# Split operands for the channel sums, a stacked gate product, and first terms on ScalarE in a two-block fp32 model

## The reference, cut to what matters

```python
def rwkv7_mixer(z, mu, w0, w2, a0, a2, g2, k_k, k_a, r_k, lnx_w, lnx_b):
    z = z + (z_prev - z) * mu                 # z_prev: z one token earlier
    r, k, v, w_low, a_low, g_low = split(z)   # 1024, 1024, 1024, 64, 64, 160
    ...
    g = jax.nn.sigmoid(g_low) @ g2            # 160 rows in, 1024 out
    kk = heads(k * k_k)                       # heads of 64 channels
    kk = kk / jnp.maximum(jnp.sqrt(jnp.sum(kk * kk, axis=-1, keepdims=True)), 1e-12)
    ...                                       # the recurrence gives y
    mean = jnp.mean(y, axis=-1, keepdims=True)
    var = jnp.mean(jnp.square(y - mean), axis=-1, keepdims=True)
    y = ((y - mean) * lax.rsqrt(var + GN_EPS)).reshape(b, s, c) * lnx_w + lnx_b
    bonus = (jnp.sum(r_h * k_h * r_k, axis=-1, keepdims=True) * v_h).reshape(b, s, c)
    return ((y + bonus) * g).astype(z.dtype)
```

## Time and profile before

| | |
|---|---|
| median of 3 runs | 2095.08 us (2093.43 to 2095.27) |
| profiled execution | 2095.13 us, its span 2093.2 us |
| PE busy | 2035.7 us, 97% of the span |
| POOL busy | 1102.0 us, 53% |
| DVE busy | 1212.4 us, 58% |
| ACT busy | 516.8 us, 25% |
| mean granted clock of PE | 0.986 of full speed |

### The profile page before, as it was taken

One profiled execution on the slowest core, in us unless ns is written; L12 is line 12 of the kernel. 1 busy time (PEld: TensorE's weight loads), 2 busy tenths in 40 slices (PEclk: granted clock), 3 DMA queues, 4 the chain that ended last, 5 costly groups with the idle time before them and its releaser, 6 DMA issues.

```text
span 2093.2 us, 39395 instructions
## 1 busy us (share of the span) xinstructions
PE 2035.7 (97%) x16125; PEld 1678.2 (80%) x16125; DVE 1212.4 (58%) x1559; ACT 516.8 (25%) x1111; POOL 1102.0 (53%) x857
## 2 busy tenths in 40 slices
PE   8999999999999998999998999999999999999998
PEld 6888787877877787788876888888886878888886
DVE  6888724466667664202068677777783756565423
ACT  2100002233434212313142122232223023333101
POOL 6777764634533474444546044422364756666663
PEclk9999999999999999999999999999999999999999
DMA  4333232254453422211323022111113332322231
GB/s 135 101 101 101 91 100 61 82 171 126 135 150 105 149 81 80 82 61 62 123 57 91 14 65 65 43 49 56 52 55 130 133 101 81 100 94 90 93 111 56
DMA packets 180472, 190.00 MB, mean 91 GB/s; under 512 B 8269, under 2 KB 161500, under 8 KB 180060
## 3 DMA queue, kind: packets, MB, share of 16 engines
q1 hardware_dynamic: 172288, 181.81, 27.3%
q10 hardware_dynamic: 8028, 5.94, 0.9%
HBM read 179.30 MB, written 8.44 MB: 90 GB/s over the span
## 4 chain that ended last, share of the span: by engine, by line
PE 63%; DVE 4%; DVEq 1%; ACT 1%; issue 1%; ACTq 0%
PE bank L886 8%; PE bank L888 8%; PE bank L887 8%; PE bank L1555 8%; PE bank L1516 3%; PE bank L1366 3%; PE bank L1382 2%; PE bank L1653 2%; PE bank L1384 2%; PE bank L1383 2%; PE bank L1288 1%; PE bank L1289 1%; PE bank L1290 1%; PE bank L1041 1%; PE bank L916 1%; PE bank L1043 1%
## 5 line engine op out<-in xcount | busy, mean ns | idle before, releaser
L724 POOL TENSOR_TENSOR wlo<-raws,whi 128x1024 fp32r<-128x1024 f32 (+5 forms) x312 | 678.7, 2175 | 46.5 <-issue 1.5
L722 POOL TENSOR_SCALAR whi<-raws 128x1024 fp32r<-128x1024 f32 (+5 forms) x312 | 331.6, 1063 | 324.8 <-PE bank L1043 173.0
L886 PE MATMUL bank<-hbuf,whi 128*128 128x512 f32 (+2 forms) x840 | 328.8, 391 | 0.0
L888 PE MATMUL bank<-hbuf,wlo 128*128 128x512 f32 (+2 forms) x840 | 327.7, 390 | 0.0
L887 PE MATMUL bank<-hbuf,whi 128*128 128x512 f32 (+2 forms) x776 | 302.8, 390 | 0.0
L645 POOL TENSOR_TENSOR spare<-ones 1x1 f32<-1x1 f32 x92 | 22.5, 245 | 346.7 <-PE bank L888 242.8
L886 PEld LDWEIGHTS bank<-hbuf,whi 128*128 128x128 f32 (+2 forms) x840 | 157.1, 187 | 35.2 <-POOL wlo L724 1.1
L888 PEld LDWEIGHTS bank<-hbuf,wlo 128*128 128x128 f32 (+2 forms) x840 | 157.0, 187 | 34.2
L887 PEld LDWEIGHTS bank<-hbuf,whi 128*128 128x128 f32 (+2 forms) x776 | 145.0, 187 | 31.0
L668 POOL TENSOR_SCALAR lg2L<-lg 128x128 fp32r<-128x128 f32 (+1 forms) x16 | 5.2, 327 | 225.2 <-DMA lg<-in_g 223.6
L2625 DVE TENSOR_REDUCE nmax<-bank 128x4 f32<-128x512 f32 (+3 forms) x40 | 21.1, 551 | 146.1 <-PE bank L1263 104.2
(11 more groups left out here) (529 smaller groups left out, 4711.5 us busy)
## 6 DMA issues: line engine op xcount, KB each, us to landing
adaw<-in_w_ada SPq DMA_DIRECT2D x64, 384.0 KB, 4.1
raws<-in_w_up SPq DMA_DIRECT2D x22, 1024.0 KB, 4.9
raws<-in_w_in SPq DMA_DIRECT2D x41, 512.0 KB, 4.0
raws<-in_w_in SPq DMA_DIRECT2D x18, 1024.0 KB, 5.0
raws<-in_pool_w_in SPq DMA_DIRECT2D x16, 1024.0 KB, 5.4
raws<-in_mla_w_in SPq DMA_DIRECT2D x10, 1024.0 KB, 6.4
raws<-in_pool_w_out SPq DMA_DIRECT2D x8, 1024.0 KB, 5.0
raws<-in_mla_w_out SPq DMA_DIRECT2D x8, 1024.0 KB, 5.3
```

The source lines that it names most:

```text
L722: G.tensor_scalar(h_, r_, 1.0, 1.0, ALU.mult, ALU.mult)
L724: G.tensor_tensor(l_, r_, f32(h_), ALU.subtract).then_inc(raw_split, 1)
L886: M.matmul(dst, wh, acts[k][0], start=(first and k == 0), stop=False)
L888: mm = M.matmul(dst, wl, acts[k][0], start=False, stop=(last and k == n - 1))
```

## The change

Six things are changed, all in the recurrence.

- The sums of the pairs' variances (pairs 0 to 5), bonus (pairs 1 to 6) and key squares (pairs 2 to 7) are made by two fp32r matmuls, one on the upper and one on the lower part of the operand, in place of one f32 matmul. ACT writes the upper part (`upper_sum`), POOL the lower (`lower_sum`), into the unused half of a `whi` and `wlo` buffer. The other sums stay f32.
- In POOL's order the lower parts of the variance and of the bonus stand after the pair's lora split and before its value strip. The split of the gate weights moves from before the value strip to behind it, and the lower part of the key squares follows it.
- In PE's wide part the variances move from after slice 2 to after slice 8, the key sums from 16 to 18, the gate from 20 to 22 (and pair 0's bonus with it).
- The 32 rows of the gate's second part are stacked three times, so that hi x hi, hi x lo and lo x hi are one matmul on 96 rows: `load_gate` makes four DMAs in place of two, ACT makes three sigmoids of the 32 rows in place of one, and POOL rounds stacks of 96 rows (`round_stacked`).
- ACT makes the first half of `take_product` for all pairs from 1 on.
- The maximum with 1e-12 leaves DVE: ACT makes max(x - 1e-24, 0) by a Relu and then the root of that plus 1e-24.

```diff
+            def round_stacked(x, parts, upper, rest, signal):
+                G.tensor_scalar(upper, x, 1.0, 1.0, ALU.mult, ALU.mult)
+                pool.drain()
+                G.tensor_tensor(upper[rest, :], x[rest, :], f32(upper[rest, :]), ALU.subtract)
+                pool.drain()
+                G.tensor_scalar(parts, f32(upper), 1.0, 1.0, ALU.mult, ALU.mult).then_inc(sem(signal), 1)
...
                 if p == 0:
                     pool.wait_ge(sem("lora.act"), 2)
                     round_in_place(tile(glow, 0), tile(glowH, 0), glowL[:, :], "glow.split")
-                    round_in_place(glow[0:32, S:2 * S], glowH[0:32, S:2 * S], glowL1, "glow.split")
+                    round_stacked(glow[0:96, S:2 * S], glowH[0:96, S:2 * S], glow96[0:96, :], slice(32, 64),
+                                  "glow.split")
...
+            def lower_sum(q, which, x):
+                hi, lo = sum_split(q, which)
+                pool.wait_ge(sem("sum.hi"), sum_number(q, which))
+                G.tensor_tensor(lo, x, f32(hi), ALU.subtract).then_inc(sem("sum.lo"), 1)
...
                         if ph == "rkv" and j == (0 if i else 1):
                             split_low_rank(i)
                             if i >= 2:
-                                split_gate(i - 2)
+                                lower_sum(i, "variance", gn_sq[:, :])
+                                lower_sum(i, "bonus", Rr[:, :])
+                        if ph == "rkv" and j == 1 and i >= 2:
+                            split_gate(i - 2)
+                            lower_sum(i, "key", tile(sq, 0))
...
+            def head_sums(dst, q, which):
+                hi, lo = sum_split(q, which)
+                pe.wait_ge(sem("sum.lo"), sum_number(q, which))
+                M.matmul(dst[:, :], same64[:, :], hi, start=True, stop=False)
+                return M.matmul(dst[:, :], same64[:, :], lo, start=False, stop=True)
...
-                for n, (w, x) in enumerate(((lg2H, glowH[0:32, S:2 * S]), (lg2H, glowL1),
-                                            (lg2L, glowH[0:32, S:2 * S]))):
-                    mm = M.matmul(dst[:, :], w[0:32, P:2 * P], x, start=False, stop=(n == 2))
-                mm.then_inc(sem("rk.g"), 1)
+                M.matmul(dst[:, :], lg2H[0:96, P:2 * P], glowH[0:96, S:2 * S], start=False, stop=True)\
+                    .then_inc(sem("rk.g"), 1)
...
                 lora_products(q)
-                rkv(0, 2)
+                rkv(0, 8)
                 if q >= 2:
                     variances(q - 2)
-                rkv(2, 8)
-                if q >= 2:
                     pe.wait_ge(sem("inv.dve"), q * TAKEN_ALL)
                     bonus_sums(q - 1)
                 else:
                     pe.wait_ge(sem("gt.taken"), 2)
                 rkv(8, 16)
+                rkv(16, 18)
                 if q >= 2:
                     key_norms(q)
-                rkv(16, 20)
+                rkv(18, 22)
                 if q >= 2:
                     gate(q - 2, q)
                 else:
                     bonus_sums(0)
-                rkv(20, 24)
+                rkv(22, 24)
...
+            def upper_sum(q, which, x):
+                A.copy(sum_split(q, which)[0], x).then_inc(sem("sum.hi"), 1)
...
                 A.activation(tile(sq, 0), kk[:, :], ACT.Square).then_inc(sem("rk.sq"), 1)
+                if q >= 2:
+                    act.wait_ge(sem("gn.v"), q - 1)
+                    act.drain()
+                    upper_sum(q, "key", tile(sq, 0))
...
-                A.activation(tile(sq, 1), bank[3][:, :], ACT.Sqrt).then_inc(sem("rk.nr"), 1)
+                A.activation(tile(sq, 1), bank[3][:, :], ACT.Relu, bias=key_floor)
+                act.drain()
+                A.activation(tile(sq, 1), tile(sq, 1), ACT.Sqrt, bias=key_rise).then_inc(sem("rk.nr"), 1)
...
                 if more:
                     sigmoids(q)
+                    act.drain()
+                    upper_sum(q, "variance", gn_sq[:, :])
+                    act.wait_ge(sem("rk.bon"), q)
+                    upper_sum(q, "bonus", Rr[:, :])
                     if q + 1 < PAIRS:
                         load_lora(q + 1)
                 if more:
+                    act.wait_ge(sem("rk.bon"), q)
+                    first_term(q, 1, Kr)
                     decays(q)
                     key_squares(q)
                 if q >= 2:
                     deviations(q - 2)
                 if more:
+                    act.wait_ge(sem("rk.bs"), q)
+                    first_term(q, 0, Rr)
                     key_lengths(q)
+                    act.wait_ge(sem("rk.bonus"), q - 1)
+                    act.wait_ge(sem("rk.tv"), q - 1)
+                    first_term(q, 2, vT[q % 2])
...
-                V.tensor_scalar(tile(sq, 1), tile(sq, 1), 1e-12, None, ALU.max)
-                dve.drain()
```

More of the change, by code:

```diff
@@ L34 @@
 SCAN_SCALE = 2.0 ** -20
+KEY_MIN = 1e-12
 BIG = 1e30
@@ L252, in build @@
         ones = sb("ones", [P, P])
-        same = {n: sb(f"same{n}", [P, P]) for n in (16, 32, 64)}
+        same = {n: sb(f"same{n}", [P, P]) for n in (16, 32)}
+        same64 = sb("same64", [P, P], F32R)
         upper1 = sb("upper1", [P, P])
@@ L438, in lora_bank, with sum_split, sum_number @@
             return bank[5 if q else 3]
+        def sum_split(q, which):
+            cols = slice(3 * S, 4 * S) if which == "bonus" else slice(2 * S, 3 * S)
+            return whi[(q + 1) % 2][:, cols], wlo[(q + 1) % 2][:, cols]
+        def sum_number(q, which):
+            return 3 * (q - 2) + ("variance", "bonus", "key").index(which) + 1
         def mix_slot(kind, i):
@@ L613, in _ @@
             G.memset(gneps_c[:, :], GN_EPS)
-            for n in (16, 32, 64):
+            G.memset(key_floor, -KEY_MIN ** 2)
+            G.memset(key_rise, KEY_MIN ** 2)
+            for n in (16, 32):
                 G.memset(same[n][:, :], 1.0)
+            G.memset(f32(same64[:, :]), 1.0)
             G.iota(cinv[:, :].rearrange("p (g t) -> p g t", g=4), [[0, 4], [1, PAD]], base=1, channel_multiplier=0,
@@ L1424, in key_norms @@
                     pe.wait_ge(sem("gn.q"), q - 1)
-                M.matmul(bank[3][:, :], same[64][:, :], tile(sq, 0), start=True, stop=True)\
-                    .then_inc(sem("rk.ss"), 1)
+                if q >= 2:
+                    head_sums(bank[3], q, "key").then_inc(sem("rk.ss"), 1)
+                else:
+                    M.matmul(bank[3][:, :], f32(same64[:, :]), tile(sq, 0), start=True, stop=True)\
+                        .then_inc(sem("rk.ss"), 1)
             def bonus_sums(q):
@@ L1431, in bonus_sums @@
                     pe.wait_ge(sem("gt.taken"), 2 * q + 2)
-                M.matmul(bank[6][:, :], same[64][:, :], Rr[:, :], start=True, stop=True)\
-                    .then_inc(sem("rk.bs"), 1)
+                if 1 <= q < PAIRS - 1:
+                    head_sums(bank[6], q + 1, "bonus").then_inc(sem("rk.bs"), 1)
+                else:
+                    M.matmul(bank[6][:, :], f32(same64[:, :]), Rr[:, :], start=True, stop=True)\
+                        .then_inc(sem("rk.bs"), 1)
             def variances(p):
                 pe.wait_ge(sem("gn.q"), p + 1)
-                M.matmul(bank[4][:, :], same[64][:, :], gn_sq[:, :], start=True, stop=True).then_inc(sem("gn.v"), 1)
+                if p < PAIRS - 2:
+                    head_sums(bank[4], p + 2, "variance").then_inc(sem("gn.v"), 1)
+                else:
+                    M.matmul(bank[4][:, :], f32(same64[:, :]), gn_sq[:, :], start=True, stop=True)\
+                        .then_inc(sem("gn.v"), 1)
             def gate(p, bonus_taken):
-                pe.wait_ge(sem("lg.ld"), (p + 1) * 32)
+                pe.wait_ge(sem("lg.ld"), (p + 1) * 64)
                 pe.wait_ge(sem("rk.bonus"), bonus_taken)
@@ L2100, in _ @@
                     A.activation(tile(glow, 0), tile(glow, 0), ACT.Sigmoid)
+                    for r0 in (64, 32):
+                        A.activation(glow[r0:r0 + 32, S:2 * S], glow[0:32, S:2 * S], ACT.Sigmoid)
                     A.activation(glow[0:32, S:2 * S], glow[0:32, S:2 * S], ACT.Sigmoid).then_inc(sem("lora.act"), 1)
@@ L2154, in deviations, with first_term @@
                     .then_inc(sem("gn.s"), 1)
+            def first_term(q, z, out_):
+                product_ready(STRIP0["rkv"] + q * 3 + z // 2, (1, 0, 1)[z])
+                A.activation(out_[:, :], bank[z][:, :], ACT.Copy, scale=pcol[q % 3][:, 11 + z:12 + z])\
+                    .then_inc(sem(f"rk.first{z}"), 1)
             def wide_part(q):
@@ L2189, in take_gates @@
                 take_gate(q, 1)
-            def first_term(z, out_):
-                product_ready(STRIP0["rkv"] + 3 + z // 2, (1, 0, 1)[z])
-                A.activation(out_[:, :], bank[z][:, :], ACT.Copy, scale=pcol[1][:, 11 + z:12 + z])\
-                    .then_inc(sem(f"rk.first{z}"), 1)
             def chain(p):
@@ L2226, in _ @@
             act.wait_ge(sem("rk.bs"), 1)
```

(4 more changed lines are left out.)

31 lines of the change are left out of this document (17 added, 14 removed).

## The result

The changed kernel takes **2121.18 us** (median of four executions, 2114.41 to 2123.42) against 2095.05 (2093.43 to 2095.27) of the kernel before, measured again beside it: 1.0119 times as long, 95% interval 1.0107 to 1.0131. The execution with the profile took 2114.41 us (span 2112.7), 19.3 more than the profiled one of before; the sum in the prediction was +14.0. So there are two things to explain: 5.3 us within the trace, and 6.8 us by which the median is longer than the profiled one. PE's mean granted clock was 0.985 of full speed in the profiled execution, and 0.981, 0.980 and 0.933 in the three longer ones.

A forecast was written before the change was run, and what follows sets the result against it. TensorE (PE), busy 97% of the span, was taken as the bound; pairs 3 to 7 +7.7, pair 2 +8.8, last gates -1.1, pair 1 -1.4 gave +14.0 us on 2095.08: 2109.1 us, range 2097 to 2119.

The forecast's parts named there:

- PE's savings: PE's wide parts: 0.41 us saved on each of 18 split sums, 7.4 us; eight gates save 4.5 us.
- The gate's term: PE's gate product: two matmuls fewer save 0.56 us per gate, taken between 0.45 and 0.87; eight gates 4.5 us.
- upper bound of 0.87: PE's gate: the saving per gate if the 96-row matmul has no cost for the change of row count.
- What PE waits for: Pairs 2 to 7: POOL's queue delivers the key part at t 17.65; an ordinary wide part gets 1.54 us longer.
- "work alone, unimpeded" rival: POOL's lower parts never impeded, key part at 15.7: +2.4 us, 2097.5 us in all; chance 0.12.
- the Trainium skill's rule: DVE with two SBUF inputs and GpSimd reading SBUF exclude each other: variance part at 7.4 instead of 7.0.
- Pair 2: Glow split before pair 2's key part adds 5.7 us of wait, low clock 1.6; with the ordinary 1.54, 8.8 us.
- the rival of a clock lowered in every pair: Waits lower PE's clock in every pair, 1.6 us more in each of five: 2117 us; chance 0.12.
- Pair 1 and the ends: Pair 1: PE's wait for pair 0's bonus sum shrinks and DVE gains; 1.4 us saved, between 0.5 and 3.
- What DVE saves: DVE: half of three products and the maximum go, some 3.8 us per pair; no gain while PE is the bound.
- A slack of 0.2 us before: DVE's rT for the next pair's first grams against when PE asks: 0.2 us before, about 2 us after.
- my faster rival: POOL in time, key part by t 14.2: -6.0 us, 2089 us, or 2082 without pair 2's part; chance 0.11.

The follow-up runs named there:

- experiment 1: The changed kernel with pair 1's bonus sum back behind slice 20, its place before the change: 2112.39 us, 1.0098 of the kernel before.
- The hold: POOL's split of pair 2's first weight strip waits until VectorE's log decays of pair 1 are done; on the changed kernel 2112.98 us, 1.008.
- 2: The changed kernel with the split of the gate's hidden rows (glow) ahead of pair 2's variance and bonus lower parts: 2110.91 us, 1.0076.
- 3: The changed kernel with POOL's value strip ahead of the variance and bonus lower parts: 2121.06 us, 1.0116.
- experiment 5: The changed kernel with the edits of 1, 2 and 3, POOL's value strip also held until VectorE's rT of the pair before: 2101.72 us, 1.0016.
- 8: The kernel of experiment 5 with PE's variance sum after slice 10 and bonus sum after slice 12 in pairs 2 to 7: 2092.65 us, 0.9984.
- 9: The kernel of 8 with POOL's first weight strip of pair 2 held until VectorE's log decays of pair 1 are done: 2089.8 us, 0.9972.

## Why the prediction was right and wrong

- **PE's savings.** A split sum at two stream matmuls and the gate without two of them: right in kind. The gate's term was mis-sized: 0.75 instead of 0.56, as the 96-row matmul costs no change. Its upper bound of 0.87 doesn't follow from the rows either: 1.68 less four stream matmuls, 0.91, is 0.77.
- **What PE waits for.** Right: the queue, its order, the key part at t 17.5 for 17.65, the wide part 1.4 us longer for 1.54. The "work alone, unimpeded" rival is excluded by the variance part's 2.05 us. Taken strictly, the Trainium skill's rule had the variance part at t 7.4 (row: 7.15); my middle value was 7.0.
- **Pair 2.** Right: 8.06 us of wait and 9.0 in all. PE's clock behind it was 0.51 for 3.0 us, some 1.5 us lost (predicted 1.6), and stayed at 1.00 behind the 1.58 us wait of pair 3: the rival of a clock lowered in every pair is excluded for this execution. The rows are two stretches of the kernel after:

```profile
1294.70:1298.00 3.30, 3.23 (x14) 2.74 (x15) 3.23 (x2) 1.41 (x2) 3.15 (x2) 1.00 0.20 59
1229.90:1232.90 3.00, 2.99 (x7) 2.42 (x8) 0.00 (x0) 1.41 (x2) 2.85 (x2) 0.51 0.00 0
```

- **Pair 1 and the ends** is the step that failed: "I take 1.4 saved, between 0.5 and 3". It was 2.5 lost in the profiled execution, with a wait of PE for Rr of 6.8 us that the sum didn't have. The new order alone brings such a wait (5.3 us), and in the trace of experiment 1 the old order takes it away (0.2). I followed the bonus sum to VectorE, who waits for it, but not to the slices that now came before it, the strip buffer that they free, and POOL's split that this starts. With 1.4 saved replaced by 2.5 lost the sum is 2113.0, against 2114.4 for the profiled execution. This step by itself would have left the time inside the range.
- **The scatter** took the median out of the range: it lies 6.8 us above the profiled execution, a term that the prediction put at nothing. The prediction started from a kernel whose three executions lie within 2 us, and took it that the new one would be alike. Where the 6.8 us lie stays open, since only the shortest execution of the changed kernel has a trace. The hold brings the executions together, and so does the early glow split, which leaves the collision in place (within 4 and 3 us, with five and four executions). What is on record points at PE's clock. It is lower in the longer executions, and the trace of the same kernel with the hold has it low in two places where the changed kernel's trace has it at 1.00: 0.50 behind the wait for hf in pair 1, and 0.60 behind the idle piece in pair 5, each over 3 us. By these shares that is an estimated 1 to 2 us each. No run tested this. Besides, in the twenty traces pair 0 starts between 1086.1 and 1090.5 us, ahead of all that was changed, so that single executions differ by up to 4.4 us from there.
- **What DVE saves.** "A slack of 0.2 us before" was close: the gate's saving, 0.75, came back as waits of 0.8, so there was none. "About 2 us after" was not: with PE 3 x 0.41 + 0.75 = 2.0 us faster a pair, VectorE was 0.8 late, so by this estimate it had some 1.2. Its own work did get shorter, but it waited about 4 us for ScalarE's first term of Rr, and then for POOL's subtraction. It cost nothing in the changed kernel, since POOL held PE up by more. Its 5.0 us of waits are the larger part of the 7.8 by which the kernel with POOL's order repaired (2089.8) misses the 2082 of my faster rival.

The two fastest kernels of one cluster are: with first terms, key floor, stacked gate and the hold, 2087.0 (0.9961), without the split sums; and the whole change with the edits of 1, 2, 3, 5, 8 and 9 and the r product on VectorE, 2087.9 (0.9966). Both beat the kernel before, and they can't be told apart (the first without the hold has a lower median, 2085.7, but two clusters): once the split sums have no waits for POOL, their saving of 7.4 us still doesn't show in the time. 4.2 us of waits for rT are left there. Open stays what lets PE lose 0.3 to 0.6 us more a pair in the latter than the waits show, and in the changed kernel, how much of the scatter the low clock and the pieces of "issue" idle time make.

## What to carry to other kernels

Before moving an instruction on the bounding engine, list what the ones that now come earlier release (a buffer, a strip) and what that starts on an engine whose instructions hold up those of another: the cost may lie in a pair that the edit was not about. Where PE and a second engine are within half a microsecond of each other in each round, as here, a matmul saved can be worth nothing until that engine is relieved too; try each alone and both together. When executions fall in two clusters, compare a trace of each: a collision decided by a microsecond can be removed by one wait that fixes who goes first, here at the price of some 2 us. And a profiled execution that is the shortest of its kernel says nothing of what the longer ones lose: profile a longer one too.

## What the runs showed of the hardware

- A VectorE instruction of 128x7 that reads two SBUF operands takes 0.17 us alone (pair 3 of the kernel with f32 sums) and 2.14 to 2.15 beside POOL's subtraction of 128x1024: the length is POOL's remainder, not its own. A copy of 128x8 with one operand took 2.10 beside such a subtraction (experiment 5) and 0.17 alone.
- The 96-row matmul follows 128-row ones at the stream's pitch (0.24 us); the three 32-row ones took 0.89.
- PE's granted clock was 0.50 to 0.51 (the lower of its two levels, 1.2 GHz) for 3 to 4 us behind waits of 6.8 and 8.1 us, and 1.00 behind one of 1.58. In between it is not settled by the wait before it alone: behind the wait for hf in pair 1 it was 1.00 in the changed kernel (2.37 us of wait) and 0.50 in the same kernel with the hold (2.35 us).
